# Decay rows by transfers from DRAM, and the norm groups' squares added on GpSimd, in a one-core SSD, attention and MoE block

## The reference

```python
a_cs = jnp.cumsum(jnp.moveaxis(dtc * a, 2, -1), axis=-1)
decay = jnp.exp(jnp.where(causal, a_cs[..., :, None] - a_cs[..., None, :], -jnp.inf))
scores = cb[:, :, :, None] * decay
y_diag = jnp.einsum("bcgrls,bcsgrp->bclgrp", scores, xdt)
...
yg = (y.reshape(bsz, l, D_INNER) * jax.nn.silu(z.astype(jnp.float32))).astype(jnp.float32)
yg = yg.reshape(bsz, l, SSD_GROUPS, D_INNER // SSD_GROUPS)
yg = yg * lax.rsqrt(jnp.mean(yg * yg, axis=-1, keepdims=True) + EPS)
```

## Time and profile before

| what | value |
|---|---|
| median of 3 runs | 1332.42 us (1331.93 to 1333.24) |
| the profiled execution | 1332.2 us, of which the span 1330.5 us |
| PE busy | 1293.8 us (97%), 7223 matmul instructions |
| PE weight loads | 651.9 us (49%) |
| DVE busy | 478.3 us (36%) |
| ACT busy | 344.0 us (26%) |
| POOL busy | 66.9 us (5%), 73 instructions |
| transfers | 461.86 MB, mean 347 GB/s |
| chain that ended last | PE 41%, DMA 27% of the span |

### The profile page before, as it was taken

The page is one execution under the profiler, slowest core; times in us unless marked ns, Lnnn a source line. Parts: engine busy times, 40 slices in busy tenths (PEclk is TensorE's granted clock), DMA queues, the critical chain, the costliest instruction groups (busy, mean ns, idle before and its releaser), DMA issues.

```text
span 1330.5 us, 18219 instructions
## 1 busy us (share of the span) xinstructions
PE 1293.8 (97%) x7223; PEld 651.9 (49%) x7223; DVE 478.3 (36%) x1142; ACT 344.0 (26%) x681; POOL 66.9 (5%) x73
## 2 busy tenths in 40 slices
PE   9999999999999999999999999999999999999997
PEld 6879888899995333333333323333333333333332
DVE  5868889988663211121111111111112111121112
ACT  3557767754442110111101100010011010111102
POOL 1000004512110000000000000000000000000000
PEclk9999999999999999999999999999999999999999
DMA  6332234334979999999999999999999999999996
GB/s 257 136 127 86 106 128 189 120 144 183 404 287 346 416 420 415 428 428 428 430 429 428 428 430 428 429 428 429 429 428 429 430 428 428 430 429 428 428 428 268
DMA packets 34628, 461.86 MB, mean 347 GB/s; under 512 B 3904, under 2 KB 3904, under 8 KB 5904
## 3 DMA queue, kind: packets, MB, share of 16 engines
q1 hardware_dynamic: 34288, 460.63, 83.0%
q10 hardware_dynamic: 288, 0.52, 0.1%
HBM read 460.09 MB, written 1.05 MB: 347 GB/s over the span
## 4 chain that ended last, share of the span: by engine, by line
PE 41%; DMA 27%; DVE 0%; issue 0%; SPq 0%; ACT 0%; DVEq 0%; ACTq 0%
PE bank L1484 39%; DMA ring<-wts_dram 27%; PE bank L1883 1%; PE bank L1877 1%; PE bank L1907 0%; SPq L404 0%; SPq L498 0%; DVE work L1478 0%; DVE work L1445 0%; ACT work L901 0%; DVE work L1389 0%; DVEq L104 0%; DVE work L1391 0%; ACT work L798 0%; PE bank L1867 0%
## 5 line engine op out<-in xcount | busy, mean ns | idle before, releaser
L1484 PE MATMUL bank<-ring,work 128*64 128x512 f32 (+3 forms) x2136 | 491.6, 590 | 21.2 <-DMA ring<-wts_dram 21.1
L1484 PE MATMUL bank<-work 128*64 128x512 f32 (+8 forms) x2216 | 433.6, 544 | 2.9 <-DVE work L1385 1.0
L1484 PEld LDWEIGHTS bank<-ring,work 128*64 128x64 f32 (+2 forms) x2136 | 156.9, 138 | 306.9 <-issue 263.7
L1484 PEld LDWEIGHTS bank<-work 128*64 128x64 f32 (+4 forms) x2216 | 147.2, 143 | 257.6 <-issue 246.8
L1412 DVE COPY work<-bank 128x256 f32<-128x256 f32 x30 | 12.7, 425 | 452.2 <-PE bank L1907 452.2
L1484 PE MATMUL bank<-hn_hi,split 128*128 128x256 f32 (+1 forms) x896 | 173.1, 288 | 0.9 <-DVE split L1003 0.8
L1484 PEld LDWEIGHTS bank<-hn_hi,split 128*128 128x128 f32 x896 | 141.3, 188 | 2.2 <-ACT work L781 1.0
L1484 PE MATMUL bank<-hn_lo,split 128*128 128x256 f32 (+1 forms) x448 | 127.1, 284 | 0.0
L1003 DVE TENSOR_TENSOR split<-ring,split 128x1024 fp32r<-128x1024 f32 x88 | 110.2, 1255 | 26.0 <-ACT split L604 25.7
L1389 DVE TENSOR_SCALAR work<-bank 128x512 f32<-128x512 f32 x32 | 22.1, 692 | 262.3 <-PE bank L1484 262.3
L829 ACT ACTIVATE work<-bank 128x512 f32<-128x512 f32 x31 | 18.5, 597 | 325.6 <-PE bank L1484 325.6
(11 more groups left out here) (309 smaller groups left out, 1035.2 us busy)
## 6 DMA issues: line engine op xcount, KB each, us to landing
ring<-wts_dram SPq DMA_DIRECT2D x123, 2048.0 KB, 23.4
work<-wts_dram SPq DMA_DIRECT2D x63, 2048.0 KB, 25.3
ring<-slabs_dram SPq DMA_DIRECT2D x23, 2048.0 KB, 7.3
ring<-wts_dram SPq DMA_DIRECT2D x7, 1024.0 KB, 17.3
work<-wts_dram SPq DMA_DIRECT2D x4, 1024.0 KB, 12.1
ring<-slabs_dram SPq DMA_DIRECT2D x2, 1152.0 KB, 5.1
work<-x_dram SPq DMA_DIRECT2D x3, 512.0 KB, 11.3
ring<-slabs_dram SPq DMA_DIRECT2D x1, 1536.0 KB, 12.5
```

What stands on the lines that cost most here:

```text
L1484: return pe.matmul(o, lhsT, rhs, start=start, stop=stop)
```

## The change

1. PE forms the cumulative sums once, in partitions 0 to 31 of bank 2. DVE copies these 32 rows to `AT`; `AT_hi`, `head_row` and their instructions are gone. SP stores `AT` (32 x 256) in a DRAM tensor `decay_rows` right after slab xs1.
2. For each chunk SP issues one transfer that reads the two rows (2 KB) from DRAM once per partition into one of three SBUF buffers `spread`: chunks 0 to 2 ahead of slab z1, 3 to 5 behind z2, 6 to 9 behind z3, 10 to 13 behind g0, 14 and 15 behind g1. From chunk 3 on, the spread of c waits for both differences of chunk c - 3. `acum_of` is gone; DVE's and ACT's differences read `spread`.
3. The squares of a norm group's four chunks are added on POOL: `sum_pair` ahead of zw in steps 3, 7, 11, 15, and in steps 5, 9, 13 (and after the last) `sum_group`, which is a pair and the addition of the two pairs into `ysum`. PE does one partition sum per group, after the score product of steps 5, 9, 13 and among the g units. ACT's square of chunk c >= 4 waits for the group's `ysum` instead of a partition sum. DVE's `ysum_of` is gone.

```diff
@@ sync
+            def spread_rows(c):
+                if c >= 3:
+                    sp.wait_ge(diff_ready, c - 2)
+                    sp.wait_ge(diff2_ready, c - 2)
+                rows_of = decay_rows[2 * c:2 * c + 2, :].rearrange("h t -> (h t)").partition_broadcast(P)
+                sp.dma_start(spread[:, c % 3, :, :].rearrange("p j t -> p (j t)"), rows_of).then_inc(spread_in[c % 3], 16)
...
+                if name == "z1":
+                    sp.wait_ge(x_in[1], 32)
+                    for c in range(3):
+                        spread_rows(c)
                 sp.dma_start(slab(name), slabs[:, OFF[i]:OFF[i] + n]).then_inc(slab_in[s], 16)
+                if name in SPREAD_AFTER:
+                    for c in SPREAD_AFTER[name]:
+                        spread_rows(c)
                 if name == "g0":
                     load_w1(1, 0, True)
+                elif name == "xs1":
+                    sp.wait_ge(cum_read, 1)
+                    sp.dma_start(decay_rows, AT).then_inc(x_in[1], 16)
@@ gpsimd
+            def sum_pair(i):
+                pool.wait_ge(ysq_ready, 2 * i + 2)
+                at = i % 2 * 2
+                link(pool.tensor_tensor(ysq[:, at, :], ysq[:, at, :], ysq[:, at + 1, :], ALU.add))
+
+            def sum_group(g):
+                sum_pair(2 * g + 1)
+                if g:
+                    pool.wait_ge(gsum_done, g)
+                pool.tensor_tensor(ysum, ysq[:, 0, :], ysq[:, 2, :], ALU.add).then_inc(ysum_ready, 1)
+
             for c in range(NX):
+                if c % 4 == 3:
+                    sum_pair(c // 2 - 1)
+                elif c % 4 == 1 and c > 1:
+                    sum_group(c // 4 - 1)
...
+            sum_group(GROUPS - 1)
@@ scalar
-            a.wait_ge(cum_read, 1)
-            a.activation(AT_hi[:, :], AT[:, :], ACT.Copy).then_inc(AT_hi_ready, 1)
...
-                a.wait_ge(acum_done, c + 1)
+                a.wait_ge(spread_in[c % 3], 16 * (c // 3 + 1))
...
-                    last = a.activation(decay[:, c % 2, 1, at:at + SEQ - lo], bank[4][:, lo:SEQ], ACT.Relu,
+                    last = a.activation(decay[:, c % 2, 1, at:at + SEQ - lo], spread[:, c % 3, 1, lo:SEQ], ACT.Relu,
...
-                    a.wait_ge(gsum_done, c // 2 - 1)
+                    a.wait_ge(ysum_ready, c // 4)
@@ vector
-                    last = d.tensor_scalar(decay[:, c % 2, 0, at:at + SEQ - lo], bank[2][:, lo:SEQ], As[:, col:col + 1],
+                    last = d.tensor_scalar(decay[:, c % 2, 0, at:at + SEQ - lo], spread[:, c % 3, 0, lo:SEQ], As[:, col:col + 1],
...
-                if c % 2 == 0 and c:
-                    ysum_of(c - 1)
@@ tensor
-            for i in range(4):
-                o = bank[2][i * HEADS_S:(i + 1) * HEADS_S, :]
+            o = bank[2][0:HEADS_S, :]
...
-            acum_of(0)
...
-                if c >= 3 and c % 2:
-                    gsum_of(c // 2 - 1)
+                if c > CHUNKS_PER_GROUP and c % CHUNKS_PER_GROUP == 1:
+                    gsum_of(c // CHUNKS_PER_GROUP - 1)
```

More of the change, by code:

```diff
@@ L77 @@
 NSPLIT = 3
+SPREAD_AFTER = {"z2": range(3, 6), "z3": range(6, 10), "g0": range(10, 14), "g1": range(14, 16)}
 UNIT = 4096
@@ L112, in meta_ssd_mla_moe @@
         with ExitStack() as lent:
-            for name, at, n in [("ukv_lo", 0, KKV * 2048), ("uq_lo", 2 * SLOT, KQ * 768), ("hn_lo", 3 * SLOT, KD * L), ("AT_hi", 3 * SLOT + KD * L, SEQ),
-                                ("head_row", 3 * SLOT + KD * L + SEQ, HEADS_S), ("uq_hi2", 3 * SLOT + 2464, 768), ("ckv_hi", 3 * SLOT + 3232, KKV * L), ("split0", 4 * SLOT, 2 * PIECE), ("split1", 4 * SLOT + 2 * PIECE, 2 * PIECE),
+            for name, at, n in [("ukv_lo", 0, KKV * 2048), ("uq_lo", 2 * SLOT, KQ * 768), ("hn_lo", 3 * SLOT, KD * L), ("uq_hi2", 3 * SLOT + 2464, 768), ("ckv_hi", 3 * SLOT + 3232, KKV * L), ("split0", 4 * SLOT, 2 * PIECE), ("split1", 4 * SLOT + 2 * PIECE, 2 * PIECE),
                                 ("attn_lo", 5 * SLOT, KD * SEQ), ("split2", 5 * SLOT + 2048, 2 * PIECE), ("hn_hi", IN_WORK, KD * L), ("mT_lo", IN_WORK + 7168, KD * SEQ),
@@ L150, in meta_ssd_mla_moe @@
         hn_lo = overlays["hn_lo"][:, :].rearrange("p (k t) -> p k t", k=KD)
-        AT_hi, head_row = overlays["AT_hi"], overlays["head_row"]
+        spread = ring[:, 3 * SLOT + 2464:3 * SLOT + 2464 + 3 * 2 * SEQ].rearrange("p (i j t) -> p i j t", i=3, j=2)
         hnT = w(3072, KD * L).rearrange("p (k t) -> p k t", k=KD)
@@ L193, in meta_ssd_mla_moe @@
         ysq = w(R + 4096, 1024).rearrange("p (i t) -> p i t", i=4)
+        ysum = w(R + 5120, SEQ)
         zw = w(9216, 256)
@@ L241, in meta_ssd_mla_moe @@
         dA, As = sm(304, 96), sm(400, 96)
-        AT = sm(496, 256)
+        AT = small[0:HEADS_S, 496:752]
         negA = sm(752, 32)
@@ L295, in meta_ssd_mla_moe @@
         zw_ready = sem("zw_ready")
-        diff2_ready, AT_hi_ready, AT_lo_ready = sem("diff2_ready"), sem("AT_hi_ready"), sem("AT_lo_ready")
-        acum_done, diff_ready, decay_exp, sc_ready = sem("acum_done"), sem("diff_ready"), sem("decay_exp"), sem("sc_ready")
+        diff2_ready = sem("diff2_ready")
+        spread_in = [sem(f"spread_in{i}") for i in range(3)]
+        diff_ready, decay_exp, sc_ready = sem("diff_ready"), sem("decay_exp"), sem("sc_ready")
         xtr_done, xdt_ready = sem("xtr_done"), sem("xdt_ready")
@@ L378, in norm_stage @@
             return (None, None) if u % 3 == 2 else (n // 4, n % 4)
+        decay_rows = nc.dram_tensor("decay_rows", (HEADS_S, SEQ), F32, kind="Internal").ap()
         block = ctx.enter_context(nc.Block())
@@ L1083, in _ @@
             d.wait_ge(cum_done, 1)
-            link(d.tensor_tensor(head_row[:, :], ident2[:, 0:E], ident[:, 2 * E:3 * E], ALU.add))
-            d.tensor_tensor(head_row[:, :], head_row[:, :], ident[:, 3 * E:P], ALU.add)
-            d.tensor_copy(AT[:, :], bank[2][:, 0:SEQ])
+            d.tensor_copy(AT[:, :], bank[2][0:HEADS_S, 0:SEQ])
             d.wait_ge(consts_ready, 2)
@@ L1126, in _ @@
             last.then_inc(q_roped, 1)
[L1127 to L1130, removed]
             def q_head(h):
@@ L1180, in diff_of @@
             def diff_of(c):
-                d.wait_ge(acum_done, c + 1)
+                d.wait_ge(spread_in[c % 3], 16 * (c // 3 + 1))
                 if c >= 2:
@@ L1689, in _ @@
             pv_pair(KD - 1)
[L1692 to L1701, removed]
             def xtr_of(c):
@@ L1708, in xtr_of, with gsum_of @@
                 last.then_inc(xtr_done, 1)
-            def gsum_of(i):
-                pe.wait_ge(ysum_ready, i + 1)
-                if i and i % 2 == 0:
-                    pe.wait_ge(gsum_read, i // 2)
-                mm(bank[7][:, 0:SEQ], ones[:, :], ysq[:, i % 2 * 2, :], i % 2 == 0, i % 2 == 1).then_inc(gsum_done, 1)
-            pe.wait_ge(AT_lo_ready, 1)
-            pe.wait_ge(scores_read, MH)
-            pe.wait_ge(pTa_ready, MH)
-            acum_of(0)
+            def gsum_of(g):
+                pe.wait_ge(ysum_ready, g + 1)
+                if g:
+                    pe.wait_ge(gsum_read, g)
+                mm(bank[7][:, 0:SEQ], ones[:, :], ysum).then_inc(gsum_done, 1)
             pe.wait_ge(kT_ready, MH)
@@ L1725, in _ @@
                 if 0 < c < NX - 1:
-                    acum_of(c + 1)
                     xtr_of(c + 1)
@@ L1732, in _ @@
                 if c == 0:
-                    acum_of(1)
                     xtr_of(1)
```

14 lines of the change are left out of this document (5 added, 9 removed).

## The result

The changed kernel takes 1334.63 us (median of 20 runs, 1333.49 to 1335.92), the kernel before beside it 1332.55 (20 runs). The ratio is 1.0015, 95% interval 1.0009 to 1.0022: 2.0 us slower, inside the 0.2% that I called no change, but on the other side of what I forecast (1330.8, 1.8 less). The median lies 0.13 us above the upper end of my range (1334.5). The profiled execution took 1333.91 us.

What follows compares the result with a forecast made beforehand. The tail is a weight stream whose loads wait for PE before 412 us; PE and DVE tie in the SSD phase. 1332.2 - 2.9 + 1.0 (SSD phase) + 0.3, plus 0.2 for the median: 1330.8 us, range 1325.5 to 1334.5.

Steps and rivals of the forecast that it cites:

- part 5: SSD phase: L1003 starts ahead of POOL's first operation, 0.24 us a step; +1.0 us at a third weight, ends 0 and 2.9.
- Rival B: SSD loop: POOL becomes the slowest engine, losing to L1003 and L1200 in nearly every step; 1337.0 us, chance 0.07.
- Part 4: SSD phase: ten POOL additions cost DVE 0.53 us each, +5.3 us, ends 2.0 and 7.3.
- Part 1: Cumulative sums at 63 us, made once instead of four times: 2.9 us off PE, ends 2.4 and 3.2.
- Part 2: PE in the SSD phase: dropping broadcasts and partition sums could save 7.3 us, a limit not in the sum.
- Part 3: DVE in the SSD phase: differences read from SBUF, -2.9 us; second term, square sums leave DVE, -2.4 us.
- Part 6: New waits: ACT's squares for ysum, 0; PE for the last group at the phase's end, +0.3 us, ends 0 and 1.8.
- Part 7: Transfers on SP's queue: 16 spreads and one store land in time and delay nothing needed; price 0.
- the exchange rate of one to one: Before 412 us: whatever PE gains or loses moves the weight stream and the end by as much.

Runs made afterwards that it cites:

- e1: The changed kernel without the pair additions on POOL and with group additions cut to 8 columns (output wrong); 1332.24 us, 0.9996 of the kernel before.
- e10: The changed kernel with the cumulative sums made four times again; 1335.91 us, 1.0035 of the kernel before.
- e9: The changed kernel with square sums back on DVE and DVE's low-half subtraction ahead of dt*x; 1324.47 us, 0.9944 of the kernel before.
- e11: The kernel before with only DVE's low-half subtraction moved ahead of dt*x; 1331.09 us, 0.9996 of the kernel before.
- e3: The changed kernel with DVE's square sums and the paired ones matmuls put back; 1331.13 us, 0.9988 of the kernel before.
- e2: The changed kernel with a 64x128 DVE copy added ahead of dt*x from the second step on; 1333.77 us, 1.0006 of the kernel before.
- e4: The kernel before with square sums on POOL and one ones matmul per group, broadcasts and four cumulative sums kept; 1331.23 us, 0.9992 of before.
- e6: The changed kernel with DVE's low-half subtraction L1039 moved ahead of dt*x; 1326.91 us, 0.9955 of the kernel before.

## Why the prediction was wrong

**The step that failed is part 5,** POOL's first operation coming late: the weight of a third, and the even mixture of "let in before L1200" and "L1200 first" under it. The lengths were right: I had L1003 starting 0.08 ahead, it is 0.09; I had 5.21 us for the step in which POOL loses to both, it is 5.19; I had 4.49 for the one in which it is let in before L1230, and the three group steps have 5.38 from product to product (217.83 to 223.21), less 0.45 and 0.47 for the two additions, 4.46. But POOL lost to both in 8 steps and was let in late in 3: 8 x (5.19 - 4.61) is 4.6 us where I had 1.0 in the sum and 2.9 as the upper end. Rival B had the length of the step, and I held it at 0.07 because POOL "does not lose always". That reading was of another operation. In the trace of before L562, the product zw, comes behind L1003's start in each of the 14 steps that have one; it is let in ahead of L1200 in nine of them (as at 215.74) and kept out in five (as at 220.61). The +1 was never in that place: from the second to the fifteenth it starts 0.10 to 0.45 us ahead of L1003, and each takes 0.85 us. I carried the mixture of the one over to the other, for which before had no row; in the change the +1 behind L1039 was kept out in 7 steps of 10, and in one more where it started 0.04 ahead. Why the +1 loses where zw mostly wins stays open.

**Part 4, the additions,** at 5.3, was too high. Where they meet DVE they cost 0.45 to 0.47 each, near the 0.53 I took; but this happens in three group steps (0.92 each) and one pair step (0.45), while the other pairs make L1258 only 0.04 us longer: 3.3 us in place of 5.3. And the three group steps are just those in which the +1 is let in late, which gives back 3 x 0.73 = 2.2. That leaves 1.1 us, the difference of the phases of the change and e1 (75.95 and 74.88). The Trainium skill, page "SBUF — State Buffer", section "SBUF: two separate sides", has the first comer hold the shared pair for its whole instruction. By that rule DVE would wait for the rest of each addition, 0.59 (217.83 to 218.42) and 0.67 us (218.62 to 219.29) in the rows above; it lost 0.45 and 0.47, less than the rule gives.

**Part 1** took 2.9 us and found "nothing else late". 2.87 went from PE at 63 us (3.89 to 1.02), but 0.70 comes back 7 us later as a wait for ACT's L717, and by 96 us some 1.9 is left (e10). Where the other 0.3 lies I did not settle. Behind that the 1.7 between the two traces at 96 us is also the difference of their spans (e10 and the change).

**Part 2** was right as a limit and right not to be in the sum: in the change PE's saving came to nothing, and e9 against e11 shows the broadcasts' 4.8 of it.

**Part 3, second term, failed too:** the 2.4 us for the square sums. Its first term was right: 0.89 to 0.69 for the three differences, 0.20 a step; but nobody profits, since L1039 then starts ahead of POOL. The sums, however, cost the kernel before next to nothing. From product to product (L1233) its plain steps take 4.87 or 4.88 us, five of those with a sum 4.80 or 4.81, and one 5.06 (three with the group's variance L1206 in place of a sum take 5.06 too, the short last step 3.5):

```profile
198.47 0.43 DVE L1233 TENSOR_TENSOR work<-work 128x256 f32<-128x256 f32 x1
...
203.35 0.42 DVE L1233 TENSOR_TENSOR work<-work 128x256 f32<-128x256 f32 x1
...
218.17 0.43 DVE L1233 TENSOR_TENSOR work<-work 128x256 f32<-128x256 f32 x1
```

The third row is followed by a sum, and the next product is at 222.98, 4.81 later: with the +1 further ahead, L1003 takes 1.22 for 1.37, and where zw stays out L1200 takes 1.02 for 1.55. Two runs say the same. e1 has no sums of 256 columns at all, e3 has them on DVE, and the phase of e3 is 2.05 us *shorter* (72.83 and 74.88; the ratios 0.9988 and 0.9996 overlap). And without the additions parts 3 and 5 make -2.9 - 2.4 + 11 x 0.58 = +1.1 for e1's phase, which is 3.1 longer than before: the missing 2.0 is about the size of this term.

**Part 6:** PE's wait for the last sum is 1.00 us, inside the 0.3 to 1.8 I gave, and by 284 us it has cost 0.3 net, as forecast. ACT's squares do wait 2.61 us for L588 in a group step (the ends reached to 0.7 each), but they cost no more than that the +1 comes 0.26 behind L1039 in place of 0.09. **Part 7** was right. On ACT the three differences from SBUF take 1.00 us together, 0.89 to 0.91 before from PSUM; ACT had the room.

The positions close the sum: against before, the first yv of the phase starts 1.9 us earlier (196.09 for 197.97), the last 2.3 later (272.04 for 269.75), PE's work at 284 and at 685 us is 2.6 later, and the span 1.7: the weight stream swallows 0.9, which the exchange rate of one to one had not. Since e10 against the change keeps the whole of its 1.71, I would not read a rule from that.

## What to carry to other kernels

Before making an engine faster, list who arrives at a shared resource just behind or just ahead of it, and by how much: here a lead of 0.1 us on a contended operation was a cliff, and a saving of 0.2 us upstream cost 0.6 a step. A mixture that was read for one operation is not that of another. And an operation's busy time is not what its removal gives: compare the steps that have it with those that do not. When busy shares fall on all engines and the time does not, look for one operation whose duration trebled. Try the order of two independent lines first: here it was worth more than all the work that the change removed, and it separated the two halves of the change, of which spread rows alone did better (by 0.25% with z first, by 0.11% and not clear of noise with lo first).

## What the runs showed of the hardware

POOL and DVE get in each other's way where both work on SBUF. A +1 of POOL that comes 0.1 us behind the start of one DVE instruction can be held out by it and by the next, where the two follow without a gap: with POOL waiting since 198.10, DVE began L1230 at 199.15, and 0.85 us became 2.77 or so in eight steps of the change and eleven of e1. This is no rule for every POOL operation. zw, which multiplies two operands, was let in ahead of the second DVE instruction in nine of 14 steps of before, without a gap either, and in all 14 such steps of e2 (1.55 for L1232 in each). For the +1 the exceptions are the three group steps, where the +1 at 220.42 took 1.66 and L1230 1.21. There the exponential that L1230 waits for ended only 0.08 us before L1230 began (ACT's L778, first row below), in the plain step 0.25 us before (second row); in e1's first group step, where the +1 is kept out, it is 0.26 again. That this let POOL in is argued, not tested, and e4 speaks against it: at 228.77 its +1 gets in late in the same way, 1.96 with 1.21 for L1217, though the exponential had ended 0.46 us before.

```profile
220.67 0.55 ACT L778 ACTIVATE work<-work 128x416 f32<-128x416 f32 x1
```
```profile
198.35 0.55 ACT L778 ACTIVATE work<-work 128x416 f32<-128x416 f32 x1
```

The rows of e4, POOL, then DVE:

```profile
228.77 1.96 POOL L575 TENSOR_SCALAR work<-work 128x256 f32<-128x256 f32 x1 [1.44 <-ACT work L775]
```
```profile
229.95 1.21 DVE L1217 TENSOR_TENSOR work<-work 128x832 f32<-128x832 f32 x1
```

One DVE instruction with a PSUM source in between was enough to let the +1 in (e6). A start 0.1 us ahead sufficed in every step of before; at 0.04 ahead POOL was let in at once in some steps and kept out in others (0.85 and 1.96 us in e4, 2.89 in the change at 255.51). I had not expected the outcome to be so regular, nor that a copy of 0.29 us added to DVE in 14 steps would leave the kernel no slower.
